# Four modulation sums of the second layer moved from the first layer's expert values to its queries

## The reference

```python
def second_block(x, c, ctx, c_ctx, ada_w, ada_b, ...):
    silu_c, silu_cc = jax.nn.silu(c), jax.nn.silu(c_ctx)
    for i in range(DEPTH_2):                       # two layers
        mod_x = jnp.split((silu_c @ ada_w[i] + ada_b[i])[:, None, :], 6, axis=-1)
        mod_c = jnp.split(silu_cc @ ada_w[i] + ada_b[i], 6, axis=-1)
        hx = modulate_2(x, norm_mix[i], mod_x[0], mod_x[1])     # shift, scale
        hc = modulate_2(ctx, norm_mix[i], mod_c[0], mod_c[1])
        ...                                        # layer 0: MLA mixer, layer 1: differential attention
        x = x + mod_x[2] * yx
        hx = modulate_2(x, norm_ffn[i], mod_x[3], mod_x[4])
        ...                                        # peer: queries, key scores, top 16, hidden, values
        x = x + mod_x[5] * y
```

## Time and profile before

| What | Value |
|---|---|
| median of 3 runs (lowest, highest) | 3320.55 us (3320.46, 3329.16) |
| profiled execution: its own time | 3321.39 us |
| profiled execution: span, mean granted clock | 3319.5 us, 0.983 |
| busy: PE, DVE, ACT, POOL | 3176.7, 2481.6, 1466.8, 1063.9 us |
| moved by DMA | 835.27 MB, mean 252 GB/s |

### The profile page before, as it was taken

The page is one execution under the profiler, slowest core; times in us unless marked ns, Lnnn a source line. Parts: engine busy times, 40 slices in busy tenths (PEclk is TensorE's granted clock), DMA queues, the critical chain, the costliest instruction groups (busy, mean ns, idle before and its releaser), DMA issues.

```text
span 3319.5 us, 52879 instructions
## 1 busy us (share of the span) xinstructions
PE 3176.7 (96%) x20142; PEld 2920.0 (88%) x20142; DVE 2481.6 (75%) x4079; ACT 1466.8 (44%) x1864; POOL 1063.9 (32%) x706
## 2 busy tenths in 40 slices
PE   7999889999999999999999999999988999999999
PEld 5998689856777899999999999998868898989998
DVE  6877568686764479878849999897665797757777
ACT  5434444322443333366633333334234567874443
POOL 0110000010000278877763335551000698721110
PEclk9999899999999999999999999999998999999999
DMA  8984157461012267799999999994203578999996
GB/s 321 333 307 171 47 190 251 160 228 61 4 39 102 94 228 273 267 323 384 380 393 393 379 377 411 409 409 175 93 1 120 183 237 300 386 370 333 351 350 231
DMA packets 305610, 835.27 MB, mean 252 GB/s; under 512 B 22432, under 2 KB 185504, under 8 KB 254368
## 3 DMA queue, kind: packets, MB, share of 16 engines
q1 hardware_dynamic: 180096, 534.82, 44.3%
q0 software_dynamic: 67968, 247.49, 19.3%
q10 hardware_dynamic: 57376, 50.72, 4.5%
HBM read 750.10 MB, written 82.84 MB: 251 GB/s over the span
## 4 chain that ended last, share of the span: by engine, by line
PE 82%; DVE 5%; DMA 5%; ACT 3%; POOL 2%; issue 1%; SPq 1%; another core or an unknown queue 0%; ACTq 0%; DVEq 0%; POOLq 0%
PE ps L3377 16%; PE ps L2936 11%; PE ps L862 7%; PE ps L3360 6%; PE ps L2912 5%; PE ps L1688 5%; PE ps L873 4%; PE ps L3362 3%; PE ps L2310 3%; DMA gates<-arena 3%; PE ps L2914 3%; PE ps L319 3%; PE ps L1430 2%; PE ps L1412 2%; POOL arena_split L2886 2%; PE ps L2150 2%
## 5 line engine op out<-in xcount | busy, mean ns | idle before, releaser
L2886 POOL TENSOR_TENSOR arena_split<-ring,arena_split 128x1024 fp32r<-128x1024 f32 x228 | 570.9, 2515 | 900.6 <-ACT arena_split L2804 898.3
L2936 PE MATMUL ps<-xT_split,arena_split 128*128 128x384 f32 x2048 | 534.0, 337 | 3.1 <-ACT xT L2834 2.6
L3377 PE MATMUL ps<-arena_split 128*128 128x384 f32 x3072 | 532.7, 334 | 2.3 <-DVE arena_split L3300 2.3
L3377 PEld LDWEIGHTS ps<-arena_split 128*128 128x128 f32 x3072 | 532.5, 188 | 2.6 <-issue 2.6
L286 DVE TENSOR_TENSOR arena_split<-ring,arena_split 128x2048 fp32r<-128x2048 f32 x128 | 292.9, 2291 | 245.1 <-ACT arena_split L280 244.3
L3271 ACT ACTIVATE arena_split<-ring 128x2048 fp32r<-128x2048 f32 x126 | 241.7, 1918 | 492.1 <-PE ps L3377 306.6
L280 ACT ACTIVATE arena_split<-ring 128x2048 fp32r<-128x2048 f32 x128 | 244.4, 1915 | 376.9 <-PE ps L862 133.3
L2936 PEld LDWEIGHTS ps<-xT_split,arena_split 128*128 128x128 f32 x2048 | 371.8, 188 | 4.2 <-issue 4.2
L3297 DVE TENSOR_TENSOR arena_split<-ring,arena_split 128x2048 fp32r<-128x2048 f32 x128 | 293.2, 2291 | 94.8 <-ACT arena_split L3271 86.6
L2912 PE MATMUL ps<-hT_split,arena_split 128*128 128x448 f32 x1024 | 338.7, 379 | 6.9 <-POOL arena_split L2886 3.9
L557 POOL DMA_DIRECT2D arena<-in_side_weights x152 | 82.8, 546 | 817.5 <-DVE arena L577 285.0
(11 more groups left out here) (355 smaller groups left out, 6339.9 us busy)
## 6 DMA issues: line engine op xcount, KB each, us to landing
ring<-in_weights SPq DMA_DIRECT2D x396, 1024.0 KB
arena<-in_side_weights POOLq DMA_DIRECT2D x152, 512.0 KB, 5.6
gates<-arena SPq DMA_DIRECT2D x76, 512.0 KB
arena<-gates SPq DMA_DIRECT2D x32, 768.0 KB
arena<-activations SPq DMA_DIRECT2D x64, 384.0 KB
activations<-xT ACTq DMA_DIRECT2D x128, 112.0 KB
arena<-gates SPq DMA_DIRECT2D x32, 448.0 KB
arena<-activations SPq DMA_DIRECT2D x64, 224.0 KB
```

The lines of the kernel that those rows point to most:

```text
L2886: pool.tensor_tensor(low, self.raw(f)[:, j, :], high.bitcast(F32), ALU.subtract)\
L2936: mm = pe.matmul(k.ps[:, j, 0:self.T], self.u[:, 2 * (f % 2) + j, a, t * P:(t + 1) * P], self.h[b][:, t, :], start=n == 0, stop=n == 3 * D ...
L3377: mm = pe.matmul(k.ps[:, t, self.from_token:self.from_token + self.T], self.v[:, f % 2, a, j * D + t * P:j * D + (t + 1) * P], self.weight ...
```

## The change

The group `SECOND` is cut in two. `SECOND` keeps vectors 0 and 1 (16 tiles, 32 steps) and stays in `PeerValues` of layer 0. A new group `REST` has vectors 2 to 5 (32 tiles, 32 steps) and is made in `PeerQuery` of layer 0: after each of the eight places where a low part is made (none at places 0 and 1), VectorE runs four side steps. POOL loads the 32 tiles from the start of that stage, then stores the four sums to a new DRAM tensor (`park`) and waits for the stores. `PeerScores`' ScalarE waits for the first store, since that sum lies where the scores are written. POOL loads the four sums back (`reload`) at the start of layer 1's `diff_qkv`, to the places where they lay before, and `second_rest` waits for that. Tiles now carry their place in the weight tensor, as the order of loading no longer is the order in memory. One loop step is written as `2 * pairs_of` in place of 4.

```diff
@@ SideModulation.__init__
-        self.buffers = [wide(22528, 4), wide(22528, 4), wide(4096, 2) + wide(14336, 2), wide(19456, 4)]
+        self.buffers = [wide(22528, 4), wide(22528, 4), wide(4096, 2) + wide(14336, 2), wide(24576, 4),
+                        wide(19456, 4)]
         self.sums = [wide(26624, 4) + context + [lru], context + wide(26624, 4),
-                     wide(24576, 6), own + context[1:] + wide(25600, 5)]
+                     wide(24576, 6), wide(12288, 1) + [lru] + wide(28672, 2), own + context[1:] + wide(25600, 1)]
+        self.back = wide(26624, 4)
...
-                       [(1, m, (1, 2) if m < 2 else (1,)) for m in range(6)]]
+                       [(1, m, (1,)) for m in range(2, 6)],
+                       [(1, m, (1, 2)) for m in range(2)]]
...
+    def park(self, pool):
+        for i, total in enumerate(self.totals[self.REST]):
+            pool.wait_ge(self.steps.sem, self.steps.at(total[3]))
+            pool.dma_start(self.k.side_dram[:, i, :], self.sums[self.REST][i]).then_inc(self.parked[i > 0].sem, 16)
+    def wait_parked(self, eng):
+        for signal, n in zip(self.parked, (1, 3)):
+            eng.wait_ge(signal.sem, signal.at(16 * n))
+    def reload(self, pool):
+        for i, room in enumerate(self.back):
+            pool.dma_start(room, self.k.side_dram[:, i, :]).then_inc(self.reloaded.sem, 16)
@@ SideTurn.tensor
+        if self.g == side.REST:
+            pe.wait_ge(side.reloaded.sem, side.reloaded.at(16 * 4))
...
-            total = side.sums[self.g][i]
+            total = side.back[i] if self.g == side.REST else side.sums[self.g][i]
@@ TokenProduct
+    def gpsimd(self, pool):
+        if self.reload:
+            self.k.enter(pool, self.s)
+            self.reload(pool)
@@ PeerQuery
     def vector(self, dve):
         self.k.enter(dve, self.s)
-        each_chunk(dve, 8, lambda c, r, i: self.w.low(dve, c, r))
+        if self.side:
+            self.side.begin(dve, self.side.REST)
+            for c in range(8):
+                self.w.low(dve, c, c)
+                self.side.run(self.side.total * (c + 1) // 8)
+        else:
+            each_chunk(dve, 8, lambda c, r, i: self.w.low(dve, c, r))
...
+    def gpsimd(self, pool):
+        if self.side:
+            self.k.enter(pool, self.s)
+            self.side.load(pool, self.side.REST)
+            self.side.park(pool)
+            self.side.wait_parked(pool)
@@ PeerScores.scalar
+        if self.side:
+            act.wait_ge(self.side.parked[0].sem, self.side.parked[0].at(16))
@@ PeerValues.sync
-        walk(sp, 0, self.pairs, 4, body)
+        walk(sp, 0, self.pairs, 2 * pairs_of, body)
@@ program
-        second_gain = turn(3, (0, 1), 1, layer=(1, 0))
-        second_rest = turn(3, (2, 3, 4, 5), 7, layer=(1, 1), column=SEQ)
+        second_gain = turn(side.SECOND, (0, 1), 1, layer=(1, 0))
+        second_rest = turn(side.REST, (2, 3, 4, 5), 7, layer=(1, 1), column=SEQ)
```

More of the change, by code:

```diff
@@ L167, in __init__ @@
         self.x_dram = nc.dram_tensor("x_kept", [P, DT, BOTH], F32).ap()
+        self.side_dram = nc.dram_tensor("side_kept", [P, 4, D], F32).ap()
         self.ps = ctx.enter_context(nc.psum_tensor("ps", [P, 8, 512], F32))
@@ L505 @@
 class SideModulation:
-    FIRST_BLOCK, MLA_FIRST, MLA_LATER, SECOND = range(4)
+    FIRST_BLOCK, MLA_FIRST, MLA_LATER, REST, SECOND = range(5)
     def __init__(self, k):
@@ L525, in __init__ @@
         self.steps = k.count_of("side_steps", sum(DT * len(c) for g in self.groups for _, _, c in g))
+        self.parked = [k.count_of("side_first_parked", 16), k.count_of("side_others_parked", 16 * 3)]
+        self.reloaded = k.count_of("side_reloaded", 16 * 4)
         self.work, self.totals = [], []
@@ L538, in __init__ @@
                         totals[total][3] = n_steps
-                    work.append((n_tiles, ops))
+                    tile = {None: m - 2, 0: 7 + m, 1: 13 + m}[layer] * DT + t
+                    work.append((n_tiles, tile, ops))
                     n_tiles += 1
@@ L553, in loads @@
         buffers = self.buffers[g]
-        for i, (n, _) in enumerate(self.work[g]):
+        for i, (_, tile, _) in enumerate(self.work[g]):
             if i >= 4:
-                pool.wait_ge(self.steps.sem, self.steps.at(self.work[g][i - 4][1][-1][4]))
-            pool.dma_start(self.like(buffers[i % 4], buffers[i % 4]), self.k.io["side_weights"][n])\
+                pool.wait_ge(self.steps.sem, self.steps.at(self.work[g][i - 4][2][-1][4]))
+            pool.dma_start(self.like(buffers[i % 4], buffers[i % 4]), self.k.io["side_weights"][tile])\
                 .then_inc(self.loaded[i % 4].sem, 16)
             yield
+    def park(self, pool):
[8 more added lines that the diff above has]
+            pool.dma_start(room, self.k.side_dram[:, i, :]).then_inc(self.reloaded.sem, 16)
     def like(self, flat, other):
@@ L566, in steps @@
         def steps():
-            for i, (n, ops) in enumerate(self.work[g]):
+            for i, (n, _, ops) in enumerate(self.work[g]):
                 w = self.buffers[g][i % 4]
@@ L579, in steps @@
                     yield
-        self.todo, self.total = steps(), sum(len(ops) for _, ops in self.work[g])
+        self.todo, self.total = steps(), sum(len(ops) for _, _, ops in self.work[g])
         self.done = 0
@@ L1644, with __init__ @@
 class TokenProduct(Stage):
-    def __init__(self, k, name, n_k, tiles, lhs, out, at=None, norm=None, steps={}, norm_rows={}, chain=None):
-        self.norm, self.steps, self.norm_rows = norm, steps, norm_rows
+    def __init__(self, k, name, n_k, tiles, lhs, out, at=None, norm=None, steps={}, norm_rows={}, chain=None,
+                 reload=None):
+        self.norm, self.steps, self.norm_rows, self.reload = norm, steps, norm_rows, reload
         self.chain = chain or (norm and norm.chain)
@@ L2265, in diff_stages @@
                             10: ([("roots", 1)], [("scale", 1)]), 11: ([], [("rotate", 1)])},
-                     norm_rows={0: 1, 1: 3}),
+                     norm_rows={0: 1, 1: 3}, reload=second_rest.side.reload),
     ]
@@ L2286, with __init__ @@
 class PeerQuery(Stage):
-    def __init__(self, k, l, T, h, queries):
-        self.k, self.s, self.T, self.h, self.q = k, k.stage(), T, h, queries
+    def __init__(self, k, l, T, h, queries, side=None):
+        self.k, self.s, self.T, self.h, self.q, self.side = k, k.stage(), T, h, queries, side
         self.w = SplitWeights(k, FIRST[f"peer{l}_q"], 8, 16384)
@@ L2335, in vector, with __init__ @@
         self.k.enter(dve, self.s)
-        each_chunk(dve, 8, lambda c, r, i: self.w.low(dve, c, r))
-        self.finish(dve, (self.copied, 8), *([(self.kept, 16)] if self.kept else []))
+        if self.side:
[5 more added lines that the diff above has]
+            each_chunk(dve, 8, lambda c, r, i: self.w.low(dve, c, r))
+        self.finish(dve, (self.copied, 8), *([(self.kept, 16)] if self.kept else []))
+    def gpsimd(self, pool):
[4 more added lines that the diff above has]
+            self.side.wait_parked(pool)
 class PeerScores(Stage):
-    def __init__(self, k, l, n, high, queries, scores):
+    def __init__(self, k, l, n, high, queries, scores, side):
         self.k, self.s, self.g, self.n, self.q, self.scores = k, k.stage(), FIRST[f"peer{l}_keys"], n, queries, scores
+        self.side = side
         self.products = k.count_of("peer_scores", n)
@@ L3334, in gpsimd @@
             work, loads = self.side.work[self.side.SECOND], self.side.loads(pool, self.side.SECOND)
-            ends = np.cumsum([len(ops) for _, ops in work]).tolist()
+            ends = np.cumsum([len(ops) for _, _, ops in work]).tolist()
             issued = 0
@@ L3451, in peer_stages @@
     scores = k.room(work, T // P, 2 * PEER_HEADS, P)
-    before = [Norm(k, [p[:4] for p in parts], high, after=gate), PeerQuery(k, l, T, (high, k.hT_split[:, :, 0:T]), queries),
-              PeerScores(k, l, T // P, high, queries, scores)]
+    before = [Norm(k, [p[:4] for p in parts], high, after=gate), PeerQuery(k, l, T, (high, k.hT_split[:, :, 0:T]), queries, side),
+              PeerScores(k, l, T // P, high, queries, scores, side)]
     hidden = PeerHidden(k, l, T - (SPREAD if l else GATHERED), scores, work)
```

## The result

The changed kernel takes 3333.45 us (median of 20 runs, 3327.6 to 3344.37), the kernel before 3321.41 us (median of 20 runs, 3317.1 to 3332.17). The ratio is 1.0038, 95% interval 1.0029 to 1.0046: 12 us slower, where 9.1 were forecast and the range ended at 3333. Sorted, the changed kernel's 20 runs lie 10.5 to 14.2 us above the 20 of the kernel before, the fastest 10.5, as a loss would have it that comes in every execution.

A forecast was written before the change was run, and what follows sets the result against it. TensorE, busy 96% of the span, was taken to bound the kernel; 0 us removed, a 7.0 us stall and 2.1 us of half clock added 9.1 us to 3320.55, giving 3329.6 us, range 3324 to 3333.

The forecast's parts named there:

- What bounds the kernel, and that the values give nothing back: TensorE bounds, busy 96% of the span; taking 38.8 us of VectorE and 16.8 MB from layer 0's values removes 0 us.
- Where the loss lies: Layer 0's queries: one TensorE wait ahead of the third chunk, 4 to 8 us, half clock behind, no further gap.
- The size of the stall: TensorE's wait in the queries for chunk 2's low part behind eight side steps: 7.0 us, bounds 4.0 and 7.8.
- the burst in full traffic: Upper bound for the queries' stall: fourth tile lands 10.8 us after issue, eighth takes 4.3 us; stall 7.8 us.
- The Trainium skill's rule on queues: At the queries' start, first tile through only about when x_kept is; stall at the upper bound, sum 10 us.
- The half clock: TensorE at 1.2 GHz after the queries' stall: 2.1 us lost, bounds 0 and 2.5.
- The sum: Stall plus half clock in the queries: 7.0 + 2.1 = 9.1 us, bounds 4.0 and 10.3.
- The case: Main case, stall and half clock in the queries: 4.0 to 10.3 us slower, chance 0.68.
- the loads don't pace the chunks: Rival it judges: side-tile loads pace every chunk of the queries, 4 us more, 13 us slower; chance 0.17 with another second wait.
- Faster: Rival: less DMA and VectorE traffic shortens the values' matmuls by up to 41 us, 3310 and below; chance 0.04.
- The short stall: Rival: transfers interleave well in the queries, stall 4.0 us or less, clock holds; 0 to 4 us, chance 0.11.
- Costed at 0: Parking stores after the queries and the reload at layer 1's start: 0 us, with 15 and 25 us cover for parking.

The follow-up runs named there:

- e3: Changed kernel with vectors 2 to 5 of the second layer not made at all (no tiles, steps, stores, reload); ratio 1.0001 to the kernel before.
- e4: Changed kernel with four side steps instead of eight ahead of chunk 2's low part, 28 behind later low parts; ratio 1.0010 to the kernel before.
- e5: Changed kernel with the store of x behind the sixth chunk, four steps ahead, four behind each low part, eight behind the last; ratio 1.0010 to before.
- e6: e5 with the side tiles of layer 0's values loaded from the third pair on, steps from the fifth; ratio 1.0002 to the kernel before.
- e1: Changed kernel with no side step ahead of chunk 2's low part, all 32 behind the low parts of chunks 2 to 7; ratio 1.0012 to before.
- e2: Changed kernel with the 2 MB store of x issued later, behind a chunk instead of at the queries' start; ratio 1.0027 to the kernel before.
- e7: Kernel before the change with the values' side tiles loaded from the third pair on, steps from the fifth; ratio 1.0006 to the kernel before.
- e8: Kernel before the change, unchanged, profiled once more; one run, 3319.5 us.

## Why the prediction came out as it did

- *What bounds the kernel, and that the values give nothing back:* right. e3 is at 1.0001, the values' matmuls take 532.7 us in e4, e5 and e6 as before, and in the changed profile they do once the half clock at their start is taken out.
- *Where the loss lies:* right. One wait ahead of the third chunk, released by L287, half clock behind it, none at the five chunks that follow; e1 takes most of the loss away, e6 all of it.
- *The size of the stall:* the step that failed. The prediction put it at "nearer to the burst in full traffic; I take 7.0 us", with 7.8 as its upper bound; it was 9.2. The landing in that bound held: the fourth tile landed 10.9 us after issue, against 10.8 in the burst; so taking less than the bound was the first error. The bound itself was 1.45 us short. The next tile on the chain took 4.9 us instead of 4.3, and the bound left out what stands between its terms: 0.29 us before POOL's first issue, 0.28 from a step's end to the load that it lets go, some 0.2 where steps follow one another. What lay beside the loads was a 2 MB store that started within 0.3 us of them, worth 3.9 us of the stall (e2); the row was from a burst beside steady traffic.
- *The Trainium skill's rule on queues:* by the Trainium skill, "DMA: Bandwidth & Descriptors", section "Queues, rings and completion order", each DMA engine takes turns between its queues packet by packet; from this and from the packets of the earlier trace rows the prediction drew a first tile that is through only about when x_kept is. The trace agrees: x_kept, issued within 0.3 us of the first load, landed after 8.1 us instead of 6.4, the first tile after 8.6, and with the store moved away (e2) after 3.6. The sum of 10 us that stood beside that rule was nearer to the 11.9 measured than the 9.1 taken.
- *The half clock:* 2.7 us behind the wait, forecast 2.1 with 2.5 as its bound; some 0.3 of it isn't clock, as e4 has it at full clock. In the queries the clock fell behind waits of 4.6 and 9.2 us and stayed full behind those of 0.2 to 2.0 (e1, e4), one profile each. That only the longer waits bring it down isn't shown for other places: 2.4 us did at the turn of the tokens, in six of ten profiles.
- *The sum:* 9.1 forecast, 11.9 measured in the profile and 12.0 between the medians. The case held 0.68 of the chance, but its bounds were too narrow by 1.6 us, and a loss beyond the 10 us that the prediction asked for was given 0.37. The range ended 0.45 us too early. The base moved as well: the kernel before is at 3321.41 over 20 runs, where the prediction had 3320.55 from three.
- *Rivals:* the loads don't pace the chunks at four steps each, and do so slightly at five or six (e1). Faster didn't come, for the reason given. The short stall, 4.0 us or less, didn't come even with the store moved: 4.6 in e2.
- *Costed at 0:* borne out for the parking, whose wait on ScalarE left no idle time of its own (the first copy of scores waits 0.36 us, for TensorE, 0.34 before), and for the reload, landed 4.6 to 7.4 us after issue at 2327 to 2329, long before the turn at 2512.

## What to carry to other kernels

Room on an idle engine is not only a sum over the stage. Work added ahead of an instruction on the chain has to be done by that instruction's own due time, including the first landing of its data, so lay it behind the first critical instruction and not ahead. Before costing the first load of a stage, list what else is issued in the same microsecond, and add what the load shares. And before making room in a stage, ask whether its bounding engine waits there at all: here 16.8 MB and 38.8 us were taken from a stage whose TensorE had nothing to gain.

## What the hardware showed unexpectedly

The same wait of 2.4 us ahead of the turn of the tokens left the clock full in some executions (turn of 3.84 us: before, e3, e6, e7) and brought it down in others (5.29 to 5.47 us: e8, which is the same kernel as before, and the changed kernel, e1, e2, e4, e5). The mean clock over the turn is 1.00 before and 0.71 in e8:

```profile
1141.07 3.84 PE ps L2476 x32
...
1143.00 5.29 PE ps L2476 x32
```

Two executions of one program thus differ there by 1.5 us. Larger is the wait at the start of the values, 0.3 to 7.4 us over ten profiles. Behind the five waits of 5.6 us and more the clock over the next 5.6 us was 0.50 to 0.73, behind the five of 2.3 and less 1.00. It goes with ScalarE's wait for the last store of activations just before, here in the kernel before and in the changed one:

```profile
1739.64 0.84 ACT L3243 ACTIVATE arena_split<-arena 128x768 fp32r<-128x768 f32 x1 [3.95 <-DMA activations<-arena]
...
1758.42 0.84 ACT L3290 ACTIVATE arena_split<-arena 128x768 fp32r<-128x768 f32 x1 [7.19 <-DMA activations<-arena]
```

That wait is 7.2 to 8.0 us in the five profiles where TensorE's is long, and 1.9 to 4.0 in the five others. Why the store lands late in some executions stays open: the side loads are not it, by e6 and e7, and the store was not moved by itself.
